# A two-layer hybrid decoder step: split halves of every product replaced by plain fp32, with twelve weight buffers

## The chip, the cores and the metric

The kernel is one program on one core of one Trainium2 chip. The metric is the device time of that core in microseconds. The kernel before took 1948.02 us (median of three runs, 1947.26 to 1955.48).

## The reference

One inference step of a two-layer trunk over 512 prompt rows and 8 x 4 sample rows (544 rows of 1024 channels), in fp32, with shared weights:

```
for l in (0, 1):
    h = LN(alpha*h + W_out [A(h) | B(h)])     # layer 0: gated mixing and pooling
    h = LN(alpha*h + W_out [C(h) | D(h)])     # layer 1: 31-tap and 3-tap convolutions
    h = LN(alpha*h + W_o softmax(q k^T) v)    # 4 heads, 256 memory rows; the 8 samples have K/V of their own
    h = LN(alpha*h + MoE(h))                  # 16 experts: silu(x Wg) * (x Wu), then Wd; two per row
```

The outputs are the rows of both groups, the projected memory keys and values of both layers, and the new history states. All weights come from HBM once per layer: 96 MB of expert weights per layer and some 30 MB of the rest, and 32 MB of the samples' cached keys and values.

## The kernel before, in words

All five engines run instruction lists of their own, written out by hand and joined by semaphores. Nothing is planned at run time except how many further blocks of 128 rows an expert needs (none in layer 0, one in layer 1).

**Weights.** SyncE loads every weight in units of 1 MB (128 partitions x 2048 words) in one fixed order, through a ring of `RING = 4` raw buffers. Of each unit ScalarE makes the high half (`whi`, type fp32r, a copy that rounds) and VectorE the low half (`wlo = raw - whi`). The raw buffer is free when the low half is made. The halves have rings of four as well. SyncE waits in order (`wait_release`), so a unit whose buffer isn't free holds up all that follow.

**Products.** The activations stand in SBUF as channel columns, also in two halves (`xhi`, `xlo`), that ScalarE and VectorE make one after the other from what TensorE transposed into PSUM. Each product is three fp32r matmuls into one bank: high x high, low x high, high x low. This is so in `row_product` (L543, 128 rows of output x 512), `column_product` and `half_columns` (L560 and L576, 128 x 272), `half_logits` (L589) and `expert_product` (L924, 128 x 512). The scores, the mixing of values, the pooling product and the expert products of a further block are plain fp32 already, and plain fp32 matmuls stand in the trace as two records each.

**Order on TensorE.** Keys and values of the prompt's memory for both layers (128 products of 512), then the columns of x; layer 0's mixer: `wz` (64 of 272), `wuv` (80 of 512) tile by tile between mixing, the pooling products, `wout0` (80 of 512) tile by tile between the transposes of the tile before; `wq` (128 of 272); attention: prompt scores, softmax and values tile by tile, then the samples' scores from eight cached key units, tile 0 of `w_o`, the samples' values from eight cached value units, the rest of `w_o`; router; 16 experts, each with 8 products for gate, 8 for up and 8 for down (the down product of expert c-1 stands behind gate and up of c); the combining of the experts' rows. Layer 1 has 320 products of 272 in its conv mixer, with the taps on VectorE and a part of them on GpSimd.

**Around an expert.** VectorE makes the list of an expert's rows (L1778), GpSimd starts an indirect transfer that gathers them from `h_rows` (L2177), and TensorE transposes them (L910) between the up product and the down product. VectorE's list for the next expert stands in its queue between six subtractions for weights (L1685).

**Around the convolution.** TensorE may write the next pair of banks only when VectorE has taken the one before (semaphores `glu` and `cx`, L1987), and VectorE has eleven or nine taps (L1967, L1969) and one subtraction of a weight unit between two of them.

Of the kernel before, what the change touches and what calls it, by code (L numbers as in the profile page):

```python
# [22 lines left out]
ALU = mybir.AluOpType  # L23
# [3 lines left out]
F32R = mybir.dt.float32r  # L27
# [7 lines left out]
def trunk_kernel(nc, a, outs):  # L35
# [29 lines left out]
    RING = 4  # L65
# [15 lines left out]
    UNITS, RAW, SPL, PLAIN = [], {}, {}, {}  # L81
    MOE_RAW, MOE_SPL = {}, {}
    count = {"raw": 0, "spl": 0, "plain": 0}
# [9 lines left out]
    def plan(key, dst_split, src, wait_kv=False, pieces=1):  # L93
        RAW[key] = count["raw"]
        count["raw"] += 1
        lands(pieces)
        kind = "spl" if dst_split else "plain"
        (SPL if dst_split else PLAIN)[key] = count[kind]
        count[kind] += 1
        UNITS.append(("unit", key, src, wait_kv))  # L100

    def plan_rows(name, w, quarters=range(4)):
        for q in quarters:
            plan((name, q), True, (lambda q: lambda s: [(s.rearrange("p (k n) -> p k n", k=2),
                 w[256 * q:256 * q + 256, :].rearrange("(k p) n -> p k n", p=P))])(q))

    def plan_cols(name, u, w, c0, c1):

        def src(s):
            v = s.rearrange("p (k n) -> p k n", k=KC)  # L110
            wv = w.rearrange("(k p) n -> p k n", p=P)
            if c1 == c0 + P:
                return [(v, wv[:, :, c0:c0 + 2 * P])]
            return [(v[:, :, 0:P], wv[:, :, c0:c0 + P]), (v[:, :, P:2 * P], wv[:, :, c1:c1 + P])]
        plan((name, u), True, src, pieces=1 if c1 == c0 + P else 2)

    def plan_memory(name, src_ap, wait_kv=False):
        plan(name, False, lambda s: [(s.rearrange("p (m n) -> p m n", m=MT),
# [5 lines left out]
    for l in range(DEPTH):  # L124
# [25 lines left out]
        MOE_RAW[l], MOE_SPL[l] = count["raw"], count["spl"]  # L150
        UNITS.append(("moe", l))
        count["raw"] += 6 * EXPERTS
        count["spl"] += 6 * EXPERTS
        for _ in range(6 * EXPERTS):
            lands(1)

    ring_release = []
    for u in UNITS:
        if u[0] == "unit":
            key = u[1]  # L160
            ring_release.append(("spl", SPL[key] + 1) if key in SPL else ("plain", PLAIN[key] + 1))
        else:
            ring_release += [("spl", MOE_SPL[u[1]] + j + 1) for j in range(6 * EXPERTS)]
# [4 lines left out]
    def share(semaphore, stages):  # L168

        at = 0  # L170
        for name, n in stages:
# [4 lines left out]
                   prob_exp=TILES, prob_norm=TILES, prob_tr=TILES, pt_copied=LASTT, att_mm=LASTT - 1, att_hi=TILES,  # L176
                   att_lo=TILES, sscore_mm=NB, os_copied=1, os_tr=1, wr_hi=1, wr_lo=1, 
                   lg_copied=1, lg_zeroed=1, 
                   scaled=TILES, moe_combined=TILES, out_mm=LASTT, o_mm=LASTT)
    LAYERED.update({name: EXPERTS for name in ("hit", "tok_mm", "tok", "xg_tr", "xg_hi", "xg_lo", "hid", "hid_tr", "hid_hi",  # L180
                                               "hid_lo", "ye", "silu")})
# [7 lines left out]
    for event in ("tr", "hi", "lo"):  # L189
# [10 lines left out]
    with ExitStack() as ctx:  # L200
# [47 lines left out]
        wrhi = sb("wrhi", [P, KC, ROUTE], F32R)  # L248
        wrlo = sb("wrlo", [P, KC, ROUTE], F32R)
# [64 lines left out]
        p_only = area(0, 2048, "p (k b n) -> p k b n", k=KC, b=NB)  # L314
# [9 lines left out]
        wr_rows = area(10496, KC * ROUTE, "p (k n) -> p k n", k=KC)  # L324
        xgT_hi = xhi[:, :, 0:P]
        xgT_lo = xlo[:, :, 0:P]
        hidT_hi = xhi[:, 0:4, P:2 * P]
        hidT_lo = xlo[:, 0:4, P:2 * P]
# [17 lines left out]
        hidT = area(1024, 512, "p (k n) -> p k n", k=4)  # L346
        y_hi = xhi[:, 0:4, 2 * P:4 * P]
        y_lo = xlo[:, 0:4, 2 * P:4 * P]
        hitT = xhi[:, 4:4 + (TILES + 1) // 2, 2 * P:4 * P]
# [13 lines left out]
        def wait_release(eng, i, shift=0):  # L363

            if i >= RING:
                kind, value = ring_release[i - RING]
                eng.wait_ge(sig("lo_made" if kind == "spl" else "plain_used"), value + shift)
# [19 lines left out]
        def wait_product(eng, tag, t, name):  # L387

            if t == LASTT:
                eng.wait_ge(sig("split_used"), SPL[(name, 3)] + 1)  # L390
# [3 lines left out]
        def wait_column(eng, tag, name, u, o):  # L394

            if o == 1:
                eng.wait_ge(sig("split_used"), SPL[(name, u)] + 1)
# [34 lines left out]
        def again_slot(l, unit):  # L432

            return raw[(MOE_RAW[l] + 6 * EXPERTS + unit % 4) % RING]
# [3 lines left out]
        def _(sp):  # L438
            sp.dma_start(mem_rows, a["mem_prompt"][0].rearrange("(m p) n -> p m n", p=P)).then_inc(sig("mem_landed"), 16)
            i_raw = 0  # L440
            for u in UNITS:
# [49 lines left out]
                i_raw += 6 * EXPERTS  # L491
                n = further_blocks(sp, l)
                def one_block(i):
                    e = sp.value_load(block_expert[0:1, i:i + 1] if isinstance(i, int) else block_expert[0:1, bass.ds(i, 1)], min_val=0, max_val=EXPERTS - 1)
                    for k, w in enumerate((w_gate, w_up, w_down)):
                        for q in range(2):
                            if k == 2:

                                sp.wait_ge(again(l, "used"), 2 + q + 6 * i)
                            elif isinstance(i, int):  # L500
                                wait_release(sp, i_raw + 2 * k + q)
# [4 lines left out]
                            sp.dma_start(again_slot(l, 2 * k + q)[:, :].rearrange("p (k n) -> p k n", k=src.shape[1]), src).then_inc(again(l, f"landed{q}"), 16)  # L506
# [7 lines left out]
                if l < DEPTH - 1:  # L514

                    sp.wait_ge(again(l, "used"), 1 + 6 * n)
# [3 lines left out]
        def _(pe):  # L520
            def to_columns(tag, t, m, source, ready):

                ready()
                if t >= 2:
                    pe.wait_ge(sig(tag + "_lo"), past(tag + "_lo") + t - 1)
# [5 lines left out]
            def row_product(tag, t, m, lhs_cols, pair, name, first, last):  # L531

                for q in range(4):
                    s = SPL[(name, q)]
                    if first:
                        pe.wait_ge(sig("hi_made"), s + 1)
                        pe.wait_ge(sig("lo_made"), s + 1)
                    for kk in range(2):
                        k = 2 * q + kk
                        for n, (x, w) in enumerate(((xhi, whi), (xlo, whi), (xhi, wlo))):  # L540
                            for half in range(2):
                                at = kk * 1024 + 512 * half
                                mm = pe.matmul(ps[0:m, 2 * pair + half, :], x[:, k, lhs_cols], w[s % RING][:, at:at + 512],  # L543
                                               start=(k == 0 and n == 0), stop=(k == KC - 1 and n == 2))
                    if last:
                        mm.then_inc(sig("split_used"), 1)
# [3 lines left out]
            def column_product(tag, name, u, o, pair):  # L550

                s = SPL[(name, u)]
                if o == 0:
                    pe.wait_ge(sig("hi_made"), s + 1)
                    pe.wait_ge(sig("lo_made"), s + 1)
                for k in range(KC):
                    at = k * 256 + o * P
                    for n, (x, w) in enumerate(((xhi, whi), (xlo, whi), (xhi, wlo))):
                        for half in range(2):
                            mm = pe.matmul(ps[:, 2 * pair + half, 0:MOVE], w[s % RING][:, at:at + P],  # L560
                                           x[:, k, half * MOVE:(half + 1) * MOVE],
                                           start=(k == 0 and n == 0), stop=(k == KC - 1 and n == 2))
# [1784 lines left out]
```

## Time and profile before

| | |
|---|---|
| median of three runs | 1948.02 us |
| span of the profiled execution | 1949.7 us |
| TensorE busy (matmuls) | 1591.0 us, 82% |
| VectorE, ScalarE, GpSimd busy | 1178.7, 720.8, 411.8 us |
| weight splitting: ScalarE L1308, L1151; VectorE L1685, L1481 | 366.7, 106.3; 436.7, 130.0 us |
| read from HBM, mean rate | 342.54 MB, 190 GB/s over the span |

The page gives the profiled execution by its span, from first to last instruction, and no time around it; the span is 1.7 us over the median of the runs. A matmul's end is modelled, so a matmul's length in the trace says less than the distance between the starts of two. In the views by stage the columns are: microseconds, then busy time and count for each engine (PE TensorE, PEld its weight loads, DVE VectorE, ACT ScalarE, POOL GpSimd), the granted TensorE clock as a share of full speed, the busy share of the DMA engines, and GB/s.

### The profile page before, as it was taken

Reading aid. Unit: us, or ns where it says so; the run is one execution under the profiler, and the core shown is the slowest. Engines: PE = TensorE matmul, PEld = TensorE weight load, DVE = VectorE, ACT = ScalarE, POOL = GpSimd, SP = SyncE. Lnnn points to the kernel's source line nnn. Section 1 sums busy time; section 2 is a strip of 40 time slices with the busy share of each in tenths; the row PEclk is TensorE's granted clock in tenths of the full one; section 3 lists DMA queues with packets and bytes.
Section 4 is the critical chain, followed back from the end, with each engine's and each line's share of the span. In section 5 each row is a group of like instructions: output and inputs, shape, how many; then the busy total and the mean of one; then the engine's idle time right before and its main releaser. Section 6 shows DMA issues by size and latency. Waiting matters only on the chain.

```text
span 1949.7 us, 21407 instructions
## 1 busy us (share of the span) xinstructions
PE 1591.0 (82%) x8295; PEld 1278.4 (66%) x8295; DVE 1178.7 (60%) x1285; ACT 720.8 (37%) x646; POOL 411.8 (21%) x405
## 2 busy tenths in 40 slices
PE   7989798899959999994496559898995899989860
PEld 5888478865647777773396557787673677777730
DVE  4333552341658788785779994513336787877636
ACT  4331321330236676673111112223202567666500
POOL 0101121000211001012689922300012000100006
PEclk9999798999979999997597779999998899999985
DMA  9730302066148999997411120203634699999822
GB/s 319 271 130 22 113 18 73 23 251 224 33 169 319 361 366 346 360 364 237 118 58 51 43 68 32 88 23 110 252 113 154 223 365 356 346 363 360 313 97 94
DMA packets 157539, 371.69 MB, mean 191 GB/s; under 512 B 8597, under 2 KB 38325, under 8 KB 157441
## 3 DMA queue, kind: packets, MB, share of 16 engines
q1 hardware_dynamic: 137200, 307.38, 44.9%
q0 software_dynamic: 12672, 44.76, 6.3%
q10 hardware_dynamic: 7585, 18.42, 2.6%
q8 instruction: 57, 0.93, 0.2%
q14 instruction: 25, 0.20, 0.0%
HBM read 342.54 MB, written 28.59 MB: 190 GB/s over the span
## 4 chain that ended last, share of the span: by engine, by line
PE 48%; DVE 21%; DMA 12%; issue 8%; POOL 4%; ACT 4%; ACTq 1%; DVEq 0%; SPq 0%; POOLq 0%
PE ps L543 15%; PE ps L924 10%; DMA arena<-h_rows,tok_of 6%; PE ps L560 6%; DMA raw<-in_w_gate_dram 4%; DVE arena L1969 3%; PE ps L832 3%; PE ps L847 3%; DVE arena L1967 3%; DVE wlo L1685 3%; DVE wlo L1481 2%; DVE xlo L1484 2%; ACT whi L1308 2%; PE ps L760 2%; PE ps L576 2%
## 5 line engine op out<-in xcount | busy, mean ns | idle before, releaser
L1685 DVE TENSOR_TENSOR wlo<-raw,whi 128x2048 fp32r<-128x2048 f32 x192 | 436.7, 2288 | 125.7 <-ACT whi L1308 124.9
L1308 ACT ACTIVATE whi<-raw 128x2048 fp32r<-128x2048 f32 x192 | 366.7, 1916 | 178.8 <-DMA raw<-in_w_gate_dram 86.9
L924 PE MATMUL ps<-whi,xhi 128*128 128x512 f32 x768 | 296.1, 413 | 18.2 <-issue 9.0
L924 PE MATMUL ps<-whi,xlo 128*128 128x512 f32 x768 | 287.4, 402 | 0.0
L924 PE MATMUL ps<-wlo,xhi 128*128 128x512 f32 x768 | 286.6, 400 | 0.0
L1481 DVE TENSOR_TENSOR wlo<-raw,whi 128x2048 fp32r<-128x2048 f32 x56 | 130.0, 2335 | 94.0 <-ACT whi L1151 94.0
L924 PEld LDWEIGHTS ps<-whi,xhi 128*128 128x128 f32 x768 | 147.1, 195 | 51.7 <-issue 18.0
L543 PE MATMUL ps<-whi,xhi 128*128 128x512 f32 (+1 forms) x528 | 170.1, 404 | 8.2 <-DVE wlo L1481 6.3
L924 PEld LDWEIGHTS ps<-whi,xlo 128*128 128x128 f32 x768 | 149.5, 195 | 34.1
L924 PEld LDWEIGHTS ps<-wlo,xhi 128*128 128x128 f32 x768 | 147.8, 192 | 35.6
L1484 DVE TENSOR_TENSOR xlo<-ps,xhi 128x1024 fp32r<-128x1024 f32 (+2 forms) x112 | 110.0, 983 | 97.3 <-ACT xhi L1155 34.4
L543 PE MATMUL ps<-wlo,xhi 128*128 128x512 f32 (+1 forms) x528 | 165.8, 395 | 0.0
L543 PE MATMUL ps<-whi,xlo 128*128 128x512 f32 (+1 forms) x528 | 165.4, 394 | 0.0
L560 PE MATMUL ps<-xhi,whi 128*128 128x272 f32 x544 | 119.0, 302 | 47.9 <-DVE rt L1987 46.6
L2176 POOL TENSOR_TENSOR wait_mark<-minus_half 1x1 f32<-1x1 f32 x32 | 29.1, 911 | 555.0 <-DVE tok_of L1778 541.6
L1151 ACT ACTIVATE whi<-raw 128x2048 fp32r<-128x2048 f32 x56 | 106.3, 1911 | 87.4 <-PE ps L560 61.3
L560 PEld LDWEIGHTS ps<-xhi,whi 128*128 128x128 f32 x544 | 90.5, 200 | 49.3 <-DVE rt L1987 47.9
L560 PE MATMUL ps<-xlo,whi 128*128 128x272 f32 x544 | 117.5, 299 | 0.0
L1155 ACT ACTIVATE xhi<-ps 128x1024 fp32r<-128x1024 f32 (+1 forms) x32 | 28.9, 905 | 238.5 <-PE ps L528 238.5
L560 PE MATMUL ps<-xhi,wlo 128*128 128x272 f32 x544 | 116.9, 297 | 0.0
L543 PEld LDWEIGHTS ps<-whi,xhi 128*128 128x128 f32 (+1 forms) x528 | 93.0, 180 | 36.2 <-issue 9.0
L543 PEld LDWEIGHTS ps<-whi,xlo 128*128 128x128 f32 (+1 forms) x528 | 94.0, 178 | 30.0
(319 smaller groups left out, 2347.2 us busy)
## 6 DMA issues: line engine op xcount, KB each, us to landing
raw<-in_w_gate_dram SPq DMA_DIRECT2D x66, 1024.0 KB, 7.4
raw<-in_w_up_dram SPq DMA_DIRECT2D x66, 1024.0 KB, 7.8
raw<-in_w_down_dram SPq DMA_DIRECT2D x66, 1024.0 KB, 7.4
raw<-in_cache_mem_k_dram SPq DMA_DIRECT2D x16, 1024.0 KB, 5.3
raw<-in_cache_mem_v_dram SPq DMA_DIRECT2D x16, 1024.0 KB, 5.6
expert_rows<-arena ACTq DMA_DIRECT2D x32, 512.0 KB
raw<-in_w_k_dram SPq DMA_DIRECT2D x8, 1024.0 KB, 8.6
raw<-in_w_v_dram SPq DMA_DIRECT2D x8, 1024.0 KB, 10.3
```

Of the source, the lines that this page charges most:

```text
L543: mm = pe.matmul(ps[0:m, 2 * pair + half, :], x[:, k, lhs_cols], w[s % RING][:, at:at + 512], start=(k == 0 and n == 0), stop=(k == KC - 1 ...
L560: mm = pe.matmul(ps[:, 2 * pair + half, 0:MOVE], w[s % RING][:, at:at + P], x[:, k, half * MOVE:(half + 1) * MOVE], start=(k == 0 and n == ...
L832: mm = pe.matmul(pair[0:NS, hh * NMEM:(hh + 1) * NMEM], q_only[:, j, b, :], KT[(b + 1) % 2][:, j, :], start=(b == 0 and j in (0, 4)), stop ...
L847: mm = pe.matmul(pair_flat(A_)[0:NS, hh * HD:(hh + 1) * HD], p_only[:, 2 * hh + m, b, :], vb[:, m, hh * HD:(hh + 1) * HD], start=(b == 0 a ...
L924: mm = pe.matmul(ps[:, bank + half, :], x[:, k, :], w[s][:, at:at + 512], start=(k == 0 and n == 0), stop=(k == 2 * k_unit - 1 and n == 2))
L1151: act.activation(whi[s % RING][:, :], raw[i % RING][:, :], ACT.Copy).then_inc(sig("hi_made"), 1)
L1308: act.activation(whi[s % RING][:, :], raw[r % RING][:, :], ACT.Copy).then_inc(sig("hi_made"), 1)
L1481: dve.tensor_tensor(wlo[s % RING][:, :], raw[i % RING][:, :], whi[s % RING][:, :].bitcast(F32), ALU.subtract).then_inc(sig("lo_made"), 1)
L1484: return dve.tensor_tensor(out, full, hi.bitcast(F32), ALU.subtract)
L1685: dve.tensor_tensor(wlo[s % RING][:, :], raw[r % RING][:, :], whi[s % RING][:, :].bitcast(F32), ALU.subtract).then_inc(sig("lo_made"), 1)
L1967: written["p"] = link.mark(dve.scalar_tensor_tensor(p_out, p_in, w, p_out, ALU.mult, ALU.add))
L1969: ins = dve.scalar_tensor_tensor(s_out, s_in, w, s_out, ALU.mult, ALU.add)
```

## The change

- `RING` is 12. The rings `whi` and `wlo` and the halves of x, of the router's weights and of a further block's rows are gone; each product reads `raw` and one `xT`, and is one plain fp32 matmul. A buffer is free when TensorE has used it (`unit_used`).
- All splitting instructions of ScalarE and VectorE go. A transposed tile is copied once: channels 0 to 511 by ScalarE (`low_columns`), 512 to 1023 by VectorE (`high_columns`), side by side. Outputs of the pooling product, of silu and of the short convolution go to `xT` directly.
- In attention the samples' keys are loaded and scored before the prompt's; the samples' softmax runs beside the prompt's first scores; the samples' values follow the prompt's values at once, and tile 0 of `w_o` stands behind them. `w_o` is loaded in one piece behind the cached values.
- All five tiles of x are transposed ahead of the `wv1` products (before: two ahead, three behind).
- A further block has six buffers of its own in the ring, so that its down weights need not wait for its gate product; a semaphore `further_done` frees them.

The core of the diff:

```diff
-    RING = 4
+    RING = 12
@@ order of loads
+        for b in range(NB):
+            plan_memory(("ks", l, b), a["cache_mem_k"][l, b].rearrange("m h c -> m (h c)"))
         plan_memory(("k", l), o_memk[l, 0].rearrange("m h c -> m (h c)"), True)
         plan_memory(("v", l), o_memv[l, 0].rearrange("m h c -> m (h c)"), True)
         for b in range(NB):
-            plan_memory(("ks", l, b), a["cache_mem_k"][l, b].rearrange("m h c -> m (h c)"))
-            if b >= 4:
-                plan_rows(f"wo{l}", a["w_o"][l], [b - 4])
-        for b in range(NB):
             plan_memory(("vs", l, b), a["cache_mem_v"][l, b].rearrange("m h c -> m (h c)"))
+        plan_rows(f"wo{l}", a["w_o"][l])
@@ buffers
-        whi = [sb(f"whi{i}", [P, UW], F32R) for i in range(RING)]
-        wlo = [sb(f"wlo{i}", [P, UW], F32R) for i in range(RING)]
-        xhi = sb("xhi", [P, KC, TOK], F32R)
-        xlo = sb("xlo", [P, KC, TOK], F32R)
+        xT = sb("xT", [P, KC, TOK])
+        aside = sb("aside", [P, KC, MT * P])
+        prob_s = sb("prob_s", [NS, D])
@@ TensorE, expert_product (the others likewise)
                     for q in range(2):
-                        s = (sb_ + k0 + q) % RING
-                        pe.wait_ge(sig("hi_made"), unit_value(sb_, k0 + q, i))
-                        pe.wait_ge(sig("lo_made"), unit_value(sb_, k0 + q, i))
+                        r = rb + k0 + q
+                        wait_landed(pe, r, 16 * i)
                         for kk in range(k_unit):
                             k = q * k_unit + kk
-                            for n, (x, w) in enumerate(((hi, whi), (lo, whi), (hi, wlo))):
-                                for half in range(nbanks):
-                                    at = (kk * nbanks + half) * 512
-                                    mm = pe.matmul(ps[:, bank + half, :], x[:, k, :], w[s][:, at:at + 512],
-                                                   start=(k == 0 and n == 0), stop=(k == 2 * k_unit - 1 and n == 2))
-                        mm.then_inc(sig("split_used"), 1)
+                            for half in range(nbanks):
+                                at = (kk * nbanks + half) * 512
+                                mm = pe.matmul(ps[:, bank + half, :], x[:, k, :], raw[r % RING][:, at:at + 512],
+                                               start=(k == 0), stop=(k == 2 * k_unit - 1))
+                        mm.then_inc(sig("unit_used"), 1)
@@ TensorE, attention
+                for b in range(NB):
...
+                    mm.then_inc(sig(f"sscore{l}_mm"), 1)
+                    if b + 2 < NB:
+                        key_columns(("ks", l, b + 2), b + 2)
+                    elif b + 2 == NB:
+                        key_columns(("k", l), NB)
...
                 scores(0)
                 scores(1)
+                prob_columns(0, NS, prob_s)
                 for t in range(LASTT):
-                    prob_columns(t, P)
+                    prob_columns(t + 1, P, prob)
...
-                row_product(f"o{l}", 0, P, cols(0), B_, f"wo{l}", True, False)
@@ ScalarE and VectorE, columns
-                act.activation(xhi[:, :, t * P:t * P + m], pair_chunks(C_ + t % 2)[:, :, 0:m], ACT.Copy).then_inc(sig(tag + "_hi"), 1)
+                act.activation(out[:, 0:G4, t * P:t * P + m], pair_chunks(C_ + t % 2)[:, 0:G4, 0:m], ACT.Copy).then_inc(sig(tag + "_low"), 1)
-                lo_of(xlo[:, :, t * P:t * P + m], pair_chunks(C_ + t % 2)[:, :, 0:m], xhi[:, :, t * P:t * P + m]).then_inc(sig(tag + "_lo"), 1)
+                dve.tensor_copy(out[:, G4:KC, t * P:t * P + m], pair_chunks(C_ + t % 2)[:, G4:KC, 0:m]).then_inc(sig(tag + "_high"), 1)
@@ VectorE, one expert
                     if c and c < EXPERTS - 1:
                         tokens(c + 1, i)
-                    make_lo_moe(l, own[0], i)
                     if c < EXPERTS - 2:
                         hits(c + 2, i)
-                    for kk in own[1:] + nxt[0:2]:
-                        make_lo_moe(l, kk, i)
```

## Rows read from the trace of the kernel before

**Rows 1.** Part 1 of the page: busy time, share of the span, instructions, by engine.

```profile
PE 1591.0 (82%) x8295; PEld 1278.4 (66%) x8295; DVE 1178.7 (60%) x1285; ACT 720.8 (37%) x646; POOL 411.8 (21%) x405
```

**Rows 2.** Waits of TensorE over the span: total us, times, longest us.

```profile
PE ps L528 <- POOL h L2114: 66.9, 9, 34.6
PE ps L560 <- DVE rt L1987: 46.6, 6, 11.3
PE ps L910 <- DMA arena<-h_rows,tok_of: 42.5, 16, 5.1
...
PE ps L543 <- DVE wlo L1481: 6.3, 2, 5.3
```

**Rows 3.** Busy time by stage, us from the span's start, columns as explained above.

```profile
0.00:119.00 119.00, 100.89 (x448) 82.47 (x448) 49.83 (x31) 50.03 (x35) 13.64 (x38) 0.99 0.74 268
119.00:206.00 87.00, 85.88 (x474) 71.70 (x475) 34.25 (x62) 22.49 (x27) 11.85 (x12) 0.98 0.14 49
206.00:229.00 23.00, 10.54 (x36) 6.19 (x34) 13.27 (x24) 6.42 (x12) 4.70 (x11) 0.64 0.28 92
229.00:353.00 124.00, 117.06 (x690) 101.37 (x689) 46.39 (x44) 19.06 (x21) 21.93 (x19) 0.94 0.22 72
353.00:484.00 131.00, 120.00 (x674) 84.57 (x675) 41.74 (x70) 34.54 (x63) 1.10 (x2) 0.97 0.49 170
484.00:568.00 84.00, 59.93 (x323) 44.34 (x321) 49.43 (x94) 18.55 (x19) 20.93 (x24) 0.88 0.29 100
568.00:900.00 332.00, 305.78 (x1406) 245.82 (x1406) 261.98 (x193) 221.79 (x157) 32.90 (x29) 0.96 0.95 339
900.00:960.00 60.00, 6.82 (x29) 5.65 (x30) 44.42 (x42) 11.30 (x8) 39.01 (x24) 0.52 0.51 157
960.00:1175.00 215.00, 147.44 (x1033) 143.84 (x1031) 187.70 (x268) 34.16 (x33) 147.94 (x132) 0.82 0.16 53
1175.00:1300.00 125.00, 115.76 (x692) 100.15 (x692) 47.98 (x53) 25.37 (x38) 26.51 (x28) 0.96 0.16 55
1300.00:1513.00 213.00, 178.60 (x996) 127.71 (x996) 91.13 (x163) 52.94 (x82) 22.09 (x26) 0.94 0.42 144
1513.00:1848.00 335.00, 307.17 (x1406) 246.84 (x1406) 264.04 (x199) 222.11 (x157) 32.46 (x29) 0.96 0.93 337
1848.00:1950.00 102.00, 35.10 (x95) 17.71 (x95) 46.53 (x48) 2.03 (x3) 36.73 (x32) 0.67 0.28 97
```

**Rows 4.** Timeline (start us, length us), TensorE, 512-column fp32r stream of an expert.

```profile
699.65 0.40 PE L924 MATMUL ps<-wlo,xhi 128*128 128x512 f32 x1
...
702.44 0.40 PE L924 MATMUL ps<-wlo,xhi 128*128 128x512 f32 x1
```

**Rows 5.** Timeline, TensorE, 272-column fp32r stream.

```profile
964.54 0.30 PE L576 MATMUL ps<-xhi,wlo 128*128 128x272 f32 x1
...
966.05 0.30 PE L576 MATMUL ps<-xhi,wlo 128*128 128x272 f32 x1
```

**Rows 6.** Timeline, weight loads of the plain 512-column stream of the further block.

```profile
1879.22 0.19 PEld L1014 LDWEIGHTS ps<-raw,arena 128*128 128x128 f32 x1 [0.24 <-issue]
...
1884.37 0.19 PEld L1014 LDWEIGHTS ps<-raw,arena 128*128 128x128 f32 x1 [0.24 <-issue]
```

**Rows 7.** Timeline, TensorE, plain 256-column stream of the samples' values.

```profile
453.73 27.81 PE L847 MATMUL ps<-raw,arena 128*32 128x256 f32 x128 [0.97 <-DVE arena L1675]
```

**Rows 8.** Timeline of VectorE, then GpSimd, at one expert's gather.

```profile
692.35 2.28 DVE L1685 TENSOR_TENSOR wlo<-raw,whi 128x2048 fp32r<-128x2048 f32 x1
...
692.51 2.16 POOL L2176 TENSOR_TENSOR wait_mark<-minus_half 1x1 f32<-1x1 f32 x1 [18.28 <-DVE tok_of L1778]
```

**Rows 9.** The tile `h_rows`: time from a transfer's issue to its landing.

```profile
DMA to landing us min/median/max: 4.3/7.8/10.6
```

**Rows 10.** Timeline of VectorE, a tap's sample part, with GpSimd busy and idle.

```profile
1085.47 1.31 DVE L1969 SCALAR_TENSOR_TENSOR arena<-arena,ccol 128x32 f32<-128x32 f32 x1
...
1139.40 0.24 DVE L1969 SCALAR_TENSOR_TENSOR arena<-arena,ccol 128x32 f32<-128x32 f32 x1
```

More of the change, by code:

```diff
@@ L432, in again_slot @@
         def again_slot(l, unit):
-            return raw[(MOE_RAW[l] + 6 * EXPERTS + unit % 4) % RING]
+            return raw[(FURTHER_RAW[l] + unit) % RING]
         @block.sync
@@ L529, in to_columns, with row_product @@
                 mm.then_inc(sig(tag + "_tr"), 1)
[L531 removed]
+            def row_product(tag, t, m, x, lhs_cols, pair, name, first, last):
                 for q in range(4):
[L534 removed]
+                    i = RAW[(name, q)]
                     if first:
[L536 to L537 removed]
+                        wait_landed(pe, i)
                     for kk in range(2):
                         k = 2 * q + kk
[L540 to L544, printed above, removed]
+                        for half in range(2):
+                            at = kk * 1024 + 512 * half
+                            mm = pe.matmul(ps[0:m, 2 * pair + half, :], x[:, k, lhs_cols], raw[i % RING][:, at:at + 512],
+                                           start=(k == 0), stop=(k == KC - 1))
                     if last:
[L546 removed]
+                        mm.then_inc(sig("unit_used"), 1)
                 if not last:
@@ L597, in product_then_columns @@
                 for t in range(TILES + 1):
-                    if t < TILES and (t or not odd(tag)):
+                    if t < TILES:
                         operands_ready(t)
@@ L638, in _ @@
                     pe.wait_ge(sig("hist_copied"), past("hist_copied") + 1)
-                    for t in range(2):
-                        to_columns("x", t, P, h[:, t, :], lambda: pe.wait_ge(sig("x_landed"), 32))
+                    for t in range(TILES):
+                        to_columns("x", t, rows(t), h[:, t, :], lambda: pe.wait_ge(sig("x_landed"), 32))
                 for m in range(MT):
@@ L1175, in _ @@
                 for m in range(MT):
+                    if name == "wv1" and m == 0:
+                        for t in range(TILES):
+                            low_columns("x", t, rows(t))
                     if m == 0:
@@ L1186, in _ @@
                     n += 1
-            for t in range(TILES):
-                columns_hi("x", t, rows(t))
-            for u in range(2):
-                make_hi(("wuv", u))
             act.wait_ge(sig("hist_zeroed"), past("hist_zeroed") + 1)
@@ L1464, in _ @@
                     return
-                for g in range(G4):
-                    make_hi(("wglu", g))
                 for t in range(TILES):
@@ L1636, in attention, with maxima @@
                 ins.then_inc(sig(f"q{l}_only"), 1)
-                def maxima(t, m):
+                for n in range(1, NB + 1):
+                    key_copy(l, n)
+                def maxima(t, m, pair):
                     if t < LASTT:
@@ L1664, in attention @@
[L1664 to L1673 removed]
+                maxima(LASTT, NS, A_)
@@ L2075, in _ @@
                 further(l)
-                combine(l, [("wglu", g) for g in range(G4)] if l < DEPTH - 1 else [])
+                combine(l)
         @block.gpsimd
```

646 lines of the change are left out of this document (238 added, 408 removed).

## The prediction

> **What bounds the kernel now.** I read the engine totals first, then the stages, then TensorE's waits. TensorE is busy for 1591 of 1949.7 us [rows 1]. By stage it is all but full in the mixer's products, in attention and in both expert stages (306 of 332 us, 307 of 335), half empty in the convolution, and idle while the experts' rows are combined, at the tail, and for 23 us at 206 [rows 3]. So TensorE's own work sets most of the time, and what it waits for is named: GpSimd's last step of a norm (66.9 us), VectorE between the convolution's banks (46.6), the gathers of experts' rows (42.5) [rows 2]. The expert stages also keep the DMA engines at 0.95 and 0.93 [rows 3]. The question is what a product costs in either form, and how much of the waiting hangs on the splitting.
>
> **The price of a product.** Starts in a stream of fp32r matmuls of 512 columns are (702.44 - 699.65) / 12 = 0.2325 us apart [rows 4], so a product of three costs 0.698. Plain fp32 gives two records a product; in the same shape their weight loads are (1884.37 - 1879.22) / 12 = 0.429 apart [rows 6]: 0.858 a product, 0.160 more. At 272 columns the three cost 3 x (966.05 - 964.54) / 12 = 0.378 [rows 5]. Plain at 272 is not in the trace; by 256 columns (27.81 / 128 = 0.217, [rows 7]) and by 512 its record costs 0.228 to 0.231; I take 0.229, so 0.458, 0.080 more.
>
> There are 528 + 768 products of 512 and 672 of 272 (544 in column products, 96 in half columns, 32 for logits): 1296 x 0.160 + 672 x 0.080 = 207 + 54 = 261 us more, and 4 more for the rows shared out in the further block (20 records at 0.2325 become 20 at 0.429). Gross +265 us. Against it stands what splitting makes late.
>
> The Trainium skill (TensorE: Matmul & The Clock Gate, section Back-to-back issue gap) says that a sustained stream of weight load and matmul reaches about 131 ns per matmul of 512 columns. Taken for a pass of a plain product, that would be 0.52 us a product, and the change would be worth hundreds of microseconds. No stream here comes near: the closest spacing of 512 columns is 0.2325 us [rows 4]. It is a rival below, with a small chance.
>
> **Stage by stage** (stretches of [rows 3]; + is longer):
>
> 0 to 119, keys and values: 128 products, +20.5. The first product starts 4.4 us earlier, since it need not wait for both halves (its wait for the low half is the 5.3 in [rows 2]); 1.5 of that are lost at the lower clock. Three tiles of x no longer stand alone behind these products, and small stalls on splits go: -5. Sum +10.5; I take +11.
>
> 119 to 206: 64 x 0.080 + 80 x 0.160 = +18, less 1: +17.
>
> 206 to 229: TensorE is busy for 10.5 of 23 us. In that stretch VectorE has the low halves of the pooled columns, and four weight subtractions of 2.28 us (the duration in [rows 8]), two of them ahead of the last gating. Without them the chain from the last tile is one gelu, one norm, one mixing, one gating: some 8.5 us. -14.5. At worst only the two subtractions go, -5.
>
> 229 to 353: 80 x 0.160 + 128 x 0.080 = +23; 7 us were idle and 0.06 of the clock is missing; the last tile's norm loses three subtractions ahead of it: -7. Sum +16.
>
> 353 to 484, attention: tile 0 of w_o +2.6; all other TensorE work is plain already and only changes places. Two waits around the samples' values go (-2.6), the last tile no longer holds up a stage, but the samples' masked queries are now waited for, with nothing to hide them (+2). I take 0, between -6 and +8. Cached keys are no danger: 12 buffers are filled in the stage before, where DMA is at 0.22.
>
> 484 to 568: 64 x 0.160 + 16 x 0.080 = +11.5; less 4 for the subtractions ahead of the last norm and one serial copy: +7.5.
>
> 568 to 900, experts: 1152 fp32r records x 0.2325 = 268. The stage's 332 us are these, 26 idle, 13 lost to the clock (0.04), and 25 of other TensorE work. Plain: 384 x 0.858 = 329.5, plus 25: 354.5. Of the idle 26 I leave 6, of the clock's 13 nothing. The reason is the gather. A trivial GpSimd instruction took 2.16 us while a subtraction of 2.28 ran on VectorE [rows 8], and the list itself stood behind others. After, the list is VectorE's first work in a step, issued some 2 us in; landing takes 4.3 to 10.6 us [rows 9], while the transposes come 16 x 0.858 = 13.7 us in. So it lands in time. 360: +28. DMA moved 332 x 339 GB/s = 113 MB; over 360 us that is 313 GB/s, below the 339 of now, and the ring starts with up to eight units more. TensorE is the bound, by a small margin. The stage at 1513: 335 to 361, +26.
>
> 900 to 960, combining: VectorE's four weight subtractions and five column halves go, but fetches and GpSimd's norm steps set most of the pace: -5 (0 to -15).
>
> 960 to 1175, convolution: 320 x 0.080 = +26 on TensorE, nearly all hidden, since VectorE is busy for 188 of 215 us and TensorE waits 46.6 for it. About 5 show ahead of the first banks. VectorE loses ten subtractions (23 us) and a split of the short convolution (2.4), but as long as GpSimd is busy on its taps, both slow each other (1.31 against 0.24 us for the same instruction, [rows 10]), so not all of it is time. -22, sum -17 (between -5 and -25).
>
> 1175 to 1300: as 229 to 353, +23.5 less 8.5: +15. 1300 to 1513: attention 0, then +7.5. 1848 to 1950: +4 for the sharing out, -1 for a half that goes: +3; the six buffers of the further block bring nothing, as TensorE waited for none of its loads.
>
> Sum: 11 + 17 - 14.5 + 16 + 0 + 7.5 + 28 - 5 - 17 + 15 + 7.5 + 26 + 3 = +94.5. Of the gross 265, some 170 come back. On the profiled execution 1949.7 + 94.5 = 2044; its span is 1.7 over the median, so 2043 us for the runs, 4.8% slower.
>
> **The rivals.**
>
> *The gathers stay late.* A ring of twelve lets SyncE queue more loads ahead, and the gather shares the engines with them. DMA at 0.95 speaks for it; against it, a full ring frees one unit at a time, every 3.4 us. Then 20 idle and 13 of clock return in each expert stage: +66, 2109 us. The Trainium skill (DMA: Bandwidth & Descriptors, Queues, rings and completion order) says that an engine takes turns between its queues packet by packet, which would let a gather pass a long queue of loads; no run here shows it yet, and [rows 9] neither.
>
> *More comes back.* VectorE's relief counts in full: the combining -15, the convolution -25 in place of -17, the expert stages without any wait (-12), attention -6. That is some -36: 2007 us.
>
> *It is faster.* In streams of hundreds the plain records would run closer than in the 16 of [rows 6]. The 94.5 us are 1296 products of 512 and 672 of about half, 1650 in all: 0.057 each, so it turns at 0.80 us a product, a record at 0.400 in place of 0.429. Were a plain record as cheap as an fp32r one (0.2325), products outside the expert stages would cost 528 x 0.39 + 672 x 0.21 = 347 less than in my sum; the expert stages would be held at today's by DMA, 54 less: about 1640 us. Against it, 128 plain records of 256 columns ran 0.217 apart, half of 0.429 and no less [rows 7].
>
> *The clock.* Were the lower clock kept in the convolution or after the waits, with plain products twice as dear there, it is +20 to +40 and inside the range.
>
> **How the numbers follow.** Forecast 0.70 (by itself 2020 to 2068), late gathers 0.10, more comes back 0.13, faster 0.03, near no change 0.02, other slower ones 0.02. The bounds of the single stages add to about -45 and +45 if they go together, and the range reaches toward the second case and the first: 2003 to 2095. About 0.5% (10 us) is what a measurement tells from no change. Faster 0.04, same 0.02, slower 0.94.
>
> **What would show it.** L924 in two records a product, 0.43 us apart; an expert stage of 355 to 365 us at a clock of 0.99 or more, with hardly a wait for `h_rows`; TensorE busy near 1830 us; convolution shorter by 17; the stretch at 206 down to 9 us. A wrong price of a record would break the forecast; so would waits on landed units among the experts.

## The result, and the profile after

The changed kernel takes 2040.6 us (median of 4 runs, 2037.6 to 2041.1) against 1947.7 for the kernel before (median of 4 runs, 1947.3 to 1955.5): a ratio of 1.0475, 95% interval 1.0447 to 1.0503. It is 4.75% slower. Forecast were 2043 us and 4.8%. The profiled execution has a span of 2039.2 us, 89.5 more than before; forecast were 94.5.

First the engine totals of the changed kernel, to be laid beside [rows 1].

```profile
PE 1814.7 (89%) x6329; PEld 1002.7 (49%) x6329; DVE 573.1 (28%) x1016; ACT 208.2 (10%) x357; POOL 356.2 (17%) x405
```

TensorE has fewer instructions and is busy for 224 us more; VectorE and ScalarE have lost half and more of their work. The span grew by 89.5 only, so TensorE also waits less. What it still waits for (us in total, times, longest), beside [rows 2]:

```profile
PE ps L520 <- POOL h L1924: 53.6, 6, 25.5
PE ps L548 <- DVE rt L1814: 18.8, 3, 7.3
...
PE ps L885 <- DMA arena<-h_rows,tok_of: 9.6, 2, 5.0
PE ps L601 <- DMA b_rows_s<-in_b_spatial_dram: 8.8, 1, 8.8
PE ps L1004 <- issue: 7.5, 1, 7.5
```

The wait for gathers fell from 42.5 us to 9.6: what is left is the first gather of each layer, which stays in every run here. The wait for VectorE in the convolution fell from 46.6 to 18.8. A new one has come: 8.8 us for `b_rows_s`, one of the small operands (0.6 us before). Then the stages of the changed kernel, from stretch to stretch, with the columns of [rows 3]:

```profile
0.00:140.00 140.00, 123.21 (x320) 58.57 (x321) 6.17 (x14) 13.24 (x16) 12.69 (x37) 0.98 0.72 262
...
253.00:386.00 133.00, 132.25 (x462) 80.31 (x461) 29.95 (x37) 8.13 (x15) 18.72 (x20) 1.00 0.20 64
386.00:514.00 128.00, 122.40 (x667) 80.99 (x666) 29.59 (x65) 26.90 (x59) 1.10 (x2) 0.99 0.49 165
...
607.00:963.00 356.00, 354.84 (x1020) 168.20 (x1021) 48.16 (x100) 35.15 (x48) 22.09 (x29) 0.99 0.89 302
963.00:1027.00 64.00, 9.14 (x37) 7.00 (x36) 36.51 (x39) 2.83 (x5) 30.70 (x25) 0.53 0.62 208
1027.00:1228.00 201.00, 165.57 (x709) 134.15 (x709) 157.93 (x255) 12.08 (x21) 129.87 (x131) 0.89 0.17 57
```

An expert stage is now 355 of 356 us of TensorE at a clock of 0.99. Its price can be read off the weight loads, here in that stage (start us, length us):

```profile
699.95 0.19 PEld L897 LDWEIGHTS ps<-raw,xT 128*128 128x128 f32 x1 [0.24 <-issue]
...
703.82 0.19 PEld L897 LDWEIGHTS ps<-raw,xT 128*128 128x128 f32 x1 [0.24 <-issue]
```

They are nine loads apart: (703.82 - 699.95) / 9 = 0.430 us, the 0.429 of [rows 6], now all through the stage. The loads of a column product of 272 columns, in the convolution:

```profile
1099.01 4.54 PEld L548 LDWEIGHTS ps<-xT,raw 128*128 128x128 f32 x20
```

Less the last load's own 0.19 us, 19 distances take 4.35 us: 0.229 each.

The stages are bounded by starts of products: of a stage's first, and for the queries and the experts of their last. The time went here. "Forecast" is the term of the prediction; the last three columns are experiments told below.

| stage | before | after | change | forecast | plain_split | no_low | early_list |
|---|---|---|---|---|---|---|---|
| keys and values | 119.3 | 140.0 | +20.7 | +11 | 138.0 | 115.0 | 119.5 |
| first column product to w_out | 109.8 | 112.6 | +2.8 | +2.5 | 128.5 | 96.0 | 111.1 |
| w_out and queries, layer 0 | 123.3 | 133.7 | +10.4 | +16 | 143.1 | 115.4 | 123.4 |
| attention, w_o, router 0 | 215.8 | 220.9 | +5.1 | +7.5 | 229.5 | 207.6 | 215.7 |
| experts 0 | 331.3 | 356.3 | +25.0 | +28 | 363.6 | 296.9 | 316.4 |
| combining | 61.2 | 63.2 | +2.0 | -5 | 58.2 | 56.7 | 57.2 |
| convolution | 215.0 | 200.9 | -14.1 | -17 | 218.2 | 193.3 | 213.0 |
| w_out and queries, layer 1 | 123.5 | 134.6 | +11.1 | +15 | 144.7 | 116.5 | 124.0 |
| attention, w_o, router 1 | 214.1 | 217.5 | +3.4 | +7.5 | 228.7 | 206.5 | 213.0 |
| experts 1 | 333.7 | 356.4 | +22.7 | +26 | 363.6 | 295.8 | 314.7 |
| tail | 102.8 | 103.1 | +0.3 | +3 | 102.2 | 101.3 | 102.2 |

Two terms are off by more than 6 us, keys and values and combining. The first has to do with loads and not with products; the second does in part.

The kernel before was run again beside each group of experiments; its medians there were 1948.4, 1950.6 and 1948.4 us. So differences of 2 or 3 us between groups say nothing.

### The profile page after: what moved, and what is told of

Read it like the earlier page. It is cut to its first block, busy times and chain, and to the rows that moved or that the text cites. A ratio compares the mean times of both kernels' runs of the same rounds, so it can differ in the third digit from the quotient of the medians.

```text
span 2039.2 us, 16191 instructions
## 1 busy us (share of the span) xinstructions
PE 1814.7 (89%) x6329; PEld 1002.7 (49%) x6329; DVE 573.1 (28%) x1016; ACT 208.2 (10%) x357; POOL 356.2 (17%) x405
## 4 chain that ended last, share of the span: by engine, by line
PE 81%; DVE 9%; DMA 4%; POOL 2%; issue 1%; ACTq 1%; ACT 1%; DVEq 0%; POOLq 0%
PE ps L897 33%; PE ps L533 21%; PE ps L548 8%; PE ps L754 3%; PE ps L820 3%; DVE arena L1796 3%; PE ps L561 2%; DVE arena L1794 2%; PE ps L735 2%; PE ps L885 1%; PE ps L774 1%; PE ps L800 1%; PE ps L520 1%; DMA arena<-expert_rows,slot_of 1%; DMA b_rows_s<-in_b_spatial_dram 1%
## 5 line engine op out<-in xcount | busy, mean ns | idle before, releaser
L897 PE MATMUL ps<-raw,xT 128*128 128x512 f32 x1536 | 677.1, 598 | 3.6 <-ACT xT L1246 2.0
L897 PEld LDWEIGHTS ps<-raw,xT 128*128 128x128 f32 x1536 | 288.9, 191 | 345.6 <-issue 340.7
L533 PE MATMUL ps<-raw,xT 128*128 128x512 f32 (+1 forms) x800 | 348.1, 593 | 1.1 <-ACT arena L1147 0.8
L548 PE MATMUL ps<-xT,raw 128*128 128x272 f32 x1088 | 256.4, 399 | 20.1 <-DVE rt L1814 18.8
L548 PEld LDWEIGHTS ps<-xT,raw 128*128 128x128 f32 x1088 | 210.2, 194 | 66.3 <-DVE rt L1814 20.3
L533 PEld LDWEIGHTS ps<-raw,xT 128*128 128x128 f32 (+1 forms) x800 | 137.3, 174 | 195.3 <-issue 193.4
L533 PE MATMUL ps<-raw,aside 128*128 128x512 f32 x256 | 113.6, 606 | 0.8 <-DVE aside L1370 0.8
L1924 POOL TENSOR_TENSOR h<-h,gb 128x1024 f32<-128x1024 f32 (+1 forms) x30 | 71.0, 2366 | 46.8 <-DVE h L1384 46.8
L1794 DVE SCALAR_TENSOR_TENSOR arena<-arena,ccol 128x512 f32<-128x512 f32 x81 | 63.8, 788 | 0.1
L1796 DVE SCALAR_TENSOR_TENSOR arena<-arena,ccol 128x32 f32<-128x32 f32 x81 | 63.5, 784 | 0.0
L754 PE MATMUL ps<-arena,gb 128*32 128x256 f32 x256 | 58.2, 381 | 0.0
L1266 ACT ACTIVATE arena<-ps 128x1024 f32<-128x1024 f32 x32 | 32.7, 1023 | 217.4 <-PE ps L897 217.4
## 6 DMA issues: line engine op xcount, KB each, us to landing
raw<-in_w_k_dram SPq DMA_DIRECT2D x8, 1024.0 KB, 18.9
```

Of the source, the lines that this page charges most:

```text
L548: mm = pe.matmul(ps[:, 2 * pair + half, 0:MOVE], raw[i % RING][:, at:at + P], xT[:, k, half * MOVE:(half + 1) * MOVE], start=(k == 0), sto ...
L754: mm = pe.matmul(pair[0:NS, hh * NMEM:(hh + 1) * NMEM], q_only[:, j, b, :], KT[b % 2][:, j, :], start=(b == 0 and j in (0, 4)), stop=(b == ...
L897: mm = pe.matmul(ps[:, bank + half, :], x[:, k, :], raw[r % RING][:, at:at + 512], start=(k == 0), stop=(k == 2 * k_unit - 1))
L1266: act.activation(ye[par], pair_flat(B_), ACT.Copy).then_inc(sig(f"ye{l}"), 1)
L1794: written["p"] = link.mark(dve.scalar_tensor_tensor(p_out, p_in, w, p_out, ALU.mult, ALU.add))
L1796: ins = dve.scalar_tensor_tensor(s_out, s_in, w, s_out, ALU.mult, ALU.add)
```

## The experiments

### Price and splitting apart

**plain_split** is the kernel before, splitting and all, with one plain product where three fp32r ones were:

```
-  for n, (x, w) in enumerate(((xhi, whi), (xlo, whi), (xhi, wlo))):
-      mm = pe.matmul(ps[...], x[:, k, cols], w[s % RING][:, at:at + 512], ...)
+  mm = pe.matmul(ps[...], xhi[:, k, cols].bitcast(F32), whi[s % RING][:, at:at + 512].bitcast(F32), ...)
```

> The kernel before with one thing changed: every product is one plain fp32 product of the high halves instead of three fp32r ones (the low halves are still made and waited for, but left out of the products). It holds the price of a product apart from the splitting. My theory: 265 us gross, less what waits hide: +20, +18, 0, +23, +3, +11 up to the first expert stage, +38 in each expert stage, +5 in the convolution, +23, +3, +11 behind it, 190 us in all, so about 2140 us, and the other 100 of what came back in the changed kernel is the splitting. Rival A, the splitting costs next to nothing and only the price counts: no longer than the changed kernel, 2040 to 2060. Rival B, nothing of the price is hidden: 2210.

Measured: 2121.6 us (2119.9 to 2122.8), ratio to before 1.090 (1.086 to 1.094), span 2118.2. So the price alone is +168.5 us by the spans, where I had summed 190, and taking away all that has to do with the splitting (with the ring and the order of attention) brings -79.0 from there to the changed kernel. Rival A would have had it at 2040 to 2060, rival B at 2210; both fall. Of a gross price of 265 us, 96 never show. By the table some 60 of them go in the two expert stages (384 x 0.160 = 61.4 us each, +32.3 and +29.9 measured), where late gathers had left TensorE idle and its granted clock at 0.96, and 22 in the convolution (25.6 us, +3.2 measured), where TensorE waits for VectorE.

**no_low** goes the other way: three fp32r products, but VectorE makes no low half.

```
   def make_lo(key):
-      dve.wait_ge(sig("hi_made"), s + 1)
-      dve.tensor_tensor(wlo[s % RING][:, :], raw[...], whi[...].bitcast(F32), ALU.subtract).then_inc(sig("lo_made"), 1)
+      pass            # the products read a tile of zeros
```

> The kernel before with its three fp32r products, ring of four and high halves, but no low half is ever made: the products read one tile of zeros in their place, so VectorE's subtractions and the waits for them are gone (left out: the low parts of every product). My theory: with the splitting's VectorE half gone, the stretch at 206 is 10 shorter, the convolution 30, the four stages with norms 7 each, an expert stage 25 each as the gathers are in time, combining 5: about 1825 us, between 1800 and 1860. Rival, the expert stages are held by DMA or by ScalarE's high halves and not by late gathers: they stay at 325 to 335 us each and the total is about 1880.

Measured: 1799.8 us (1796.3 to 1802.9), ratio 0.924 (0.920 to 0.927), span 1801.2, 148.5 under before. I had said 1825 and at least 1800, so it lies just under the range. Where I was too low is the expert stage: 297 us, 34 shorter and not 25. The first expert stage of no_low, with the columns of [rows 3]:

```profile
534.00:831.00 297.00, 292.52 (x1406) 239.44 (x1406) 27.80 (x67) 220.67 (x156) 22.89 (x29) 0.99 1.00 377
```

ScalarE's 221 us, nearly all high halves, are still there and hold nothing up (the rival falls); TensorE is full at 293 of 297 us, and DMA with it, at 1.00 and 377 GB/s. The stretch from the last product of w_uv to w_out is as telling: 24.4 us before, 24.6 in plain_split, 10.2 after, 10.5 in no_low. It is the low halves and nothing else.

The two runs also show that the parts don't add. Splitting costs 148 us beside fp32r products (its low halves alone). Beside plain ones all of it, with the ring and the order of attention, costs 79, and 8.6 of these are the order (first_filled, below): longer products cover part of it. The price of a plain product is 168 us with the splitting there and more without: 238 from no_low to the changed kernel, though there the high halves, the ring and the order change as well.

### The gathers

In plain_split the splitting is untouched, VectorE's subtractions stand where they stood, and still TensorE waits for the gathers 15.3 us in 4 times, not 42.5 in 16. So all but one gather in each layer, beside its first, came in time through the longer products, and did not need the freed VectorE that I had put first. **early_list** asks what lateness alone cost. It is the kernel before with the list of an expert's tokens made half a step earlier:

```
   # TensorE, step c
   expert_product(k + 2, i, 1, xgT_hi, xgT_lo, 4, 1)
+  if c < EXPERTS - 2: find_tokens(c + 2, i)      # was the last thing of the step
   # VectorE, step c
-  if c and c < EXPERTS - 1: tokens(c + 1, i)     # first thing of the step
   dve.tensor_tensor(hid, silu, ps[:, 1, :], ALU.mult)...
+  if c < EXPERTS - 2: tokens(c + 2, i)
```

> The kernel before (split halves, fp32r) with one move in the expert stages: TensorE's list of an expert's tokens is worked out after the gate and up products of the step two ahead, and VectorE reduces it right behind the gated rows, so each gather is issued more than half a step earlier. My theory: in the kernel before the late gathers cost about 20 us of idle and most of the 13 us of clock in each expert stage; with them in time a stage goes from 332 to between 303 and 315 us: about 1910 us, between 1890 and 1925. Rival, the chain of halves (high on ScalarE, low on VectorE, a ring of four) paces the expert stages: they stay at 325 or more, total 1935 to 1950.

Measured: 1912.7 us (1912.0 to 1915.8), ratio to before 0.981 (0.978 to 0.985). It beats both kernels. The waits of TensorE in it, and one expert stage:

```profile
PE ps L528 <- POOL h L2114: 61.7, 9, 30.6
PE ps L560 <- DVE rt L1987: 46.9, 6, 11.0
PE ps L924 <- issue: 16.2, 21, 2.4
...
PE ps L924 <- DVE xlo L1484: 11.1, 12, 1.9
...
PE ps L910 <- DMA arena<-h_rows,tok_of: 9.7, 2, 4.9
```

```profile
570.00:886.00 316.00, 299.21 (x1405) 238.37 (x1405) 261.35 (x192) 220.67 (x156) 17.69 (x29) 0.99 0.98 357
```

All gathers but the first of each layer are in time (16 waits before, 2 now), and the clock in the stage is 0.99 in place of 0.96, which is the rest of the theory. That it was lower behind those waits can be seen in the kernel before, in two stretches that begin where waits for gathers of 3.4 and 2.2 us end (columns of [rows 3]):

```profile
601.70:605.10 3.40, 3.40 (x13) 2.92 (x12) 3.40 (x4) 1.24 (x2) 0.00 (x0) 0.50 1.00 353
642.70:646.10 3.40, 3.15 (x12) 2.87 (x13) 1.28 (x2) 2.79 (x2) 0.00 (x0) 0.50 1.05 399
```

The stages are 15 and 19 us shorter, where I expected 17 to 29. TensorE is still idle for 17 of 316 us, and its waits ahead of L924 grow (for the low half of x 8.1 us before and 11.1 now; with the releaser "issue", behind which the profile shows nothing waited for, 9.0 and 16.2). That the chain of halves would be next is likely by this, but no run here shows it. The rival (the chain of halves paces it at 325 or more) falls.

### Twelve buffers and the small transfers

The changed kernel's first stage has a gap of 8.8 us for `b_rows_s`. The rows of ScalarE's issues and of TensorE's first instruction behind the wait, in the changed kernel's timeline:

```profile
18.81 12.72 ACTq L1123 DMA_DIRECT2D b_rows_s<-in_b_spatial_dram  x8
...
49.08 1.12 PE L601 MATMUL ps<-ident,arena 128*128 128x128 f32 x4 [8.81 <-DMA b_rows_s<-in_b_spatial_dram]
```

The last of eight loads of a few words is issued at 31.5 us, and TensorE goes on 17 us later, when it has landed. SyncE has issued twelve loads of 1 MB by then, and seven of them have not landed; one of w_k takes 18.9 us from issue to landing (median), 8.6 before and 8.5 with six buffers. Two runs take it apart.

**ring6**: six buffers, with the landing values per slot in the expert loop that go with them.

```
-  RING = 12
+  RING = 6
-  wait_landed(pe, r, 16 * i)
+  wait_landed(pe, r, 32 * i)
```

> The changed kernel with six weight buffers instead of twelve. My theory: depth buys nothing where TensorE is the bound, and twelve loads at once delay small transfers. So the wait for b_rows_s in the first stage (8.8 us) shrinks to under 2, the stage of combining gets 3 to 5 us shorter (fetches of expert rows no longer behind eight weight loads), the expert stages stay at 356 each: 2028 us, between 2022 and 2038. Rival, the depth is what keeps TensorE fed: waits on landed units appear among the experts and after a norm, +10 or more, 2050 or above.

**small_later**: twelve buffers, TensorE's transposes of the small operands one product later.

```
-  if name == "wv0":
+  if name == "wk1":
       small_operands()
```

> The changed kernel with TensorE's transposes of the small operands placed ahead of the second layer's keys instead of ahead of the first layer's values, some 27 us later. My theory: the wait of 8.8 us for b_rows_s is only its place in the order, since small transfers queue behind twelve weight loads; it goes in full, 2031 us, between 2028 and 2036, and the stage is 131 us. Rival, all transfers of the first stage are late and the wait turns up at another load: 2038 to 2042.

Measured: ring6 2032.5 us (2028.4 to 2039.4), span 2028.7; small_later 2029.7 us (2024.6 to 2034.1), span 2027.3. In both the wait is gone and the stage is 127.4 and 127.3 us: 12.7 shorter, not 8.8. The rest is the clock, as the row of small_later beside the first row of the changed kernel above shows:

```profile
0.00:127.00 127.00, 119.14 (x320) 56.66 (x320) 6.07 (x14) 13.21 (x16) 12.69 (x37) 1.00 0.79 288
```

The same 320 instructions are busy for 119.1 us in place of 123.2. But not all of that lies behind the wait. Weight loads among the first products, in the changed kernel and in ring6, and the changed kernel's stretch behind the wait with the columns of [rows 3]:

```profile
11.30 0.34 PEld L533 LDWEIGHTS ps<-raw,aside 128*128 128x128 f32 x1 [0.52 <-issue]
12.15 0.34 PEld L533 LDWEIGHTS ps<-raw,aside 128*128 128x128 f32 x1 [0.52 <-issue]
```

```profile
11.09 0.19 PEld L533 LDWEIGHTS ps<-raw,aside 128*128 128x128 f32 x1 [0.24 <-issue]
11.52 0.19 PEld L533 LDWEIGHTS ps<-raw,aside 128*128 128x128 f32 x1 [0.24 <-issue]
```

```profile
49.00:52.00 3.00, 2.92 (x10) 2.40 (x11) 1.61 (x6) 0.00 (x0) 0.00 (x0) 0.50 1.02 408
```

Until 14.7 us the changed kernel's records are 0.85 us apart, twice the 0.43 of ring6, and it comes to the small transposes 2.2 us later for it. That slow start is not the ring's: first_filled, with twelve buffers as well, does not have it, and waits 10.0 us for `b_rows_s` instead. So the landing sets when TensorE goes on, at 49.08 us against 38.12 in ring6, and 1.7 us more are lost behind it, at a granted clock of 0.50: 11.0 + 1.7 = 12.7. The rival of small_later, another late load, falls. In ring6 no wait on landed units turns up among the experts (356.2 and 356.3 us): six buffers are enough there, and the rival that the depth feeds TensorE falls too. Its combining is 5.6 us shorter (57.6, I had said 3 to 5), but the convolution, w_out with the queries and attention behind it are 2.1, 1.2 and 2.6 longer, which no run explains.

**loads_held** keeps twelve buffers and holds the convolution's first loads back while the experts' rows are combined:

```
+  if key == ("wglu", 0):
+      sp.wait_ge(sig("moe0_combined"), past("moe0_combined") + 4)
   wait_release(sp, i_raw)
```

> The changed kernel with one wait more: SyncE's loads of the convolution's first weights wait until four of five tiles of the experts' rows are combined. My theory: with twelve buffers eight weight loads start at the end of the experts, share the DMA engines with the last store of expert rows (6.7 us, 3.8 in the kernel before) and with the fetches (9.5 and 10.8 us to landing, against 6.8 to 10.7): held back, combining takes 55 to 58 us in place of 63: about 2034 us, between 2030 and 2037. Rival, the stage is paced by VectorE and GpSimd and the difference is scatter: 62 to 64 us, 2040; or the first product then waits for its weights, 2042 and above.

What it is about can be seen in two stretches, first the changed kernel, then loads_held (start us, length us; the last store of expert rows, the first fetch, the first row combined, and the third pair):

```profile
964.11 21.61 SPq L447 DMA_DIRECT2D raw<-in_w_in_cd_dram  x8
965.17 0.34 ACTq L1271 DMA_DIRECT2D expert_rows<-arena  x1
971.91 0.95 POOL L2032 DMA_INDIRECT arena<-expert_rows,slot_of  x1 [43.83 <-DMA expert_rows<-arena]
...
981.36 1.28 DVE L1747 SCALAR_TENSOR_TENSOR h<-arena,rw,h 128x1024 f32<-128x1024 f32 x1 [24.39 <-DMA arena<-expert_rows,slot_of]
...
999.44 1.28 DVE L1747 SCALAR_TENSOR_TENSOR h<-arena,rw,h 128x1024 f32<-128x1024 f32 x1 [7.93 <-DMA arena<-expert_rows,slot_of]
```

```profile
961.99 0.34 ACTq L1273 DMA_DIRECT2D expert_rows<-arena  x1
965.59 0.95 POOL L2034 DMA_INDIRECT arena<-expert_rows,slot_of  x1 [40.68 <-DMA expert_rows<-arena]
...
972.48 1.28 DVE L1749 SCALAR_TENSOR_TENSOR h<-arena,rw,h 128x1024 f32<-128x1024 f32 x1 [18.70 <-DMA arena<-expert_rows,slot_of]
...
986.79 2.55 DVE L1749 SCALAR_TENSOR_TENSOR h<-arena,rw,h 128x1024 f32<-128x1024 f32 x1 [4.16 <-DMA arena<-expert_rows,slot_of]
```

From the store to the first fetch 6.7 us fall to 3.6; from there to the first row combined 9.5 to 6.9; from there to the third pair 18.1 to 14.3. Combining takes 55.0 us in place of 63.2, the 8 expected. Only the first of the three holds in all runs, though. With twelve buffers and the loads not held, store to first fetch took 6.2 to 6.7 us in four runs; with six or four buffers, in five runs, 3.7 to 4.3. But from the first fetch to the first row it took 10.7 us in the kernel before, longer than the changed kernel's 9.5, and in prompt_first, with twelve buffers and the same early loads, 7.2: there combining took 58.4 us. With four buffers and the same code the stage took 61.2, 58.2 and 57.2 us. So some 3 us of combining are shown to be the loads', and the rest is in part scatter. But the time is 2039.3 us (2037.7 to 2043.6), no gain against the changed kernel's 2040.6: the convolution behind it grew by 5.0 (205.9), with its remaining weights now loaded into it (DMA share 0.30 in place of 0.17). TensorE is busy for 2 us more there and idle for 38 in place of 35; what of it the loads do is not settled. The time lies outside my 2030 to 2037: the theory holds for the stage in this run and fails for the whole.

### The order of attention

**prompt_first** is the changed kernel with the old order: units, key columns, scores and softmax of the prompt first, the samples' behind them. The edit moves blocks:

```
-  key_columns(("ks", l, 0), 0); ...; for b in range(NB): <sample scores>; prompt scores and values
-  prob_columns(0, NS, prob_s)          # first
+  key_columns(("k", l), 0); prompt scores and values; for b in range(NB): <sample scores>
+  prob_columns(LASTT, NS, prob_s)      # last, right ahead of the samples' values
```

> The changed kernel with the order of attention undone: prompt scores and values first, sample scores behind them (the first tile of w_o stays behind the samples' values, so nothing stands beside the samples' softmax). My theory: the order is worth only the samples' serial softmax, some 4 us in a layer: 2048 us, between 2040 and 2056. Rival, the order hides much more of the serial work (maxima, exponentials, columns, masks): 10 or more in a layer, 2060 and above. Second rival, nothing: 2040.

Measured: 2063.5 us (2061.4 to 2065.3), span 2059.5: attention with its w_o is 10.7 and 12.7 us longer. My 4 was wrong, the first rival right. TensorE's waits in the first layer's attention of prompt_first show part of the chain of maxima, exponentials and columns:

```profile
PE ps L770 <- DVE prob_s L1501: 4.8, 1, 4.8
...
PE ps L770 <- DVE arena L1501: 2.8, 1, 2.8
```

But the kernel before had the old order with a filler in that very place, tile 0 of w_o. **first_filled** puts that back as well:

```
+  row_product(f"o{l}", 0, P, xT, cols(0), B_, f"wo{l}", True, False)
   prob_columns(LASTT, NS, prob_s)
```

> The changed kernel with the old order of attention and, unlike in the run before, the old filler too: the first tile of w_o (16 plain products, 13.7 us) stands between the samples' scores and their columns. My theory: the order of the change is worth 11 us in a layer only against a chain of the samples' softmax that nothing covers; with the filler back both orders cost the same: 2042 us, between 2036 and 2048. Rival, the new order is better in itself (no serial masks and columns before the samples' values): 2050 to 2060 here too.

Measured: 2051.2 us (2048.1 to 2054.7), span 2047.8, 8.6 over the changed kernel: 1.4 us in layer 0 and 7.7 in layer 1. That is outside my 2036 to 2048 and just inside the rival's 2050 to 2060. The difference between the layers is the clock. In layer 0 of the changed kernel 16 records of the scores run 1.7 us slower than in layer 1, at a granted clock of 0.50 (the row below, columns of [rows 3]), and the way from the router's products to the first expert's is 1.7 us longer, 0.4 of it a gather's wait; in layer 1 of first_filled 16 records of the scores and the 32 of w_o's tile 1 lose 1.7 us each.

```profile
444.90:448.30 3.40, 3.40 (x10) 2.72 (x9) 0.00 (x0) 2.67 (x9) 0.00 (x0) 0.50 0.02 5
```

From the last product of the queries to the first for the router, where the order can act, it is 186.4 us in layer 1 of the changed kernel and 190.7 in layer 0 of first_filled, and neither holds such a loss. So the order is worth 4.3 us a layer, neither nothing nor the 10 of the rival.

## Why the prediction was right

**The price of a product** (0.160 and 0.080 us) was right: 0.430 us a record in the expert stages, 0.429 forecast, and 0.229 at 272 columns, the value that I had interpolated. The rival that plain records run closer in long streams is refuted by them. The spacing of about 131 ns that the Trainium skill gives (TensorE: Matmul & The Clock Gate, section Back-to-back issue gap) shows in no row read here: plain records of 512 columns stayed at 0.430 us and fp32r ones at 0.23.

**That 170 of 265 come back** was right in size (265 - 89.5 = 175), and the runs split it: about 96 us of price covered by waits and a lower clock that the kernel before had anyway, about 79 from what the splitting, the order and the ring change between plain_split and the changed kernel.

**Experts**, +28 and +26 forecast, +25.0 and +22.7 measured. Of the idle time only 1 us is left, not 6. The reason given was half right. That late gathers made the idle time and the lower clock is shown by early_list (-15 and -19 us). That VectorE's freedom was needed to bring them in time is refuted: in plain_split all but one a layer, beside the first, were in time with VectorE as loaded as ever.

**The stretch at 206**, -14.5 forecast, 24.4 to 10.2 measured; no_low and plain_split tie it to the low halves.

**Convolution**, -17 forecast, -14.1 measured; by its parts the price shows with 3.2 us (forecast 5), the rest brings -17.3 (forecast -22).

**Products with norms**: w_out and queries were forecast +16 and +15, and came to +10.4 and +11.1. From plain_split to the changed kernel they lose 9.4 and 10.1 us, not 7 to 8.5, and 2 to 3 of the gross 23 are covered.

**Attention**, +7.5 forecast in each layer, came to +5.1 and +3.4. The sum gave the new order next to nothing (two waits of 2.6 us away, 2 us of masks added); first_filled makes it 4.3 us a layer.

**The steps that failed** are the two with loads. "TensorE waited for none of its loads" was argued of the further block only, and for the ring I asked whether twelve buffers bring anything, not whether twelve loads at once delay what other queues carry. In keys and values that is 12.7 us; without it the stage is +8.0, and +11 was forecast. The sum there was wrong too: its terms, +20.5, -4.4, +1.5 and -5, add to +12.6 and not to +10.5. In combining +2.0 came for the -5 forecast: some 3 of these 7 us are shown to be the loads' (store to first fetch), six buffers took 5.6 off and holding all loads back 8.2, but prompt_first with twelve buffers was 4.8 shorter too. I had rightly named SyncE's deeper queue as a danger for the gathers, where it did no harm (3.9, 6.8 and 9.2 us to landing, against [rows 9]), and did not carry the thought to the fetches and the small loads. Of the Trainium skill's rule that an engine takes turns between its queues (DMA: Bandwidth & Descriptors, section Queues, rings and completion order) the gathers bear out the hope that I drew from it (6.8 us in the median), and the burst at the start does not (17 us for a few words). That the total still came within 3 us of the forecast (5.0 by the spans) is luck in part: these two misses, 17 us too low, stand against a gain under-sized elsewhere by 22.

## What to carry to other kernels

Price a swap of arithmetic per record from the trace, then ask stage by stage what else sets its end: here a third of the gross price never showed and another third was bought back, and still the cheaper product won. A better kernel than both needed no change of arithmetic, only a list made half a step earlier (1.9% faster); look first for a late small step behind the engine that seems the bound. When a ring gets deeper, list every small transfer that is issued while it fills, and put the instruction that waits for them later.

## What the runs showed of the hardware

Behind a wait of 8.8 us of TensorE the granted clock was 0.50 (49 to 52 us), and 1.7 us more were lost there. The first products of a run started at either rate: 0.85 us a record until 14.7 us in the changed kernel, 0.43 from the second on in ring6 and first_filled. In the first stage a load of 1 MB took 18.9 us to land (median) with twelve buffers and 8.5 with six: the depth added waiting there. With the low halves gone, the expert stage drew 377 GB/s at a DMA share of 1.00, against 339 at 0.95 before [rows 3]: the 0.95 was not a ceiling.
